# The up projection of an fp32 decoder trunk: seven products for two of every three tile pairs instead of one of two, the norm's factor moved, loops written out

## The reference, cut to what matters

```
x  = x + merged @ w_o                      # the stage before the change
h2 = rmsnorm(x) * g_ffn
f_gate, f_up = split(h2 @ w_up)            # 1024 -> 2 x 2816, the changed stage
f  = causal_depthwise_conv3(f_gate)        # along tokens
x  = x + (silu(f) * f_up) @ w_down         # the stage behind it
y  = rmsnorm(x) * g_final                  # rmsnorm(x) = x / sqrt(mean(x*x) + 1e-6)
```

## Time and profile before

| what | value |
|---|---|
| median of the runs | 860.32 us |
| the profiled execution's own time | 860.38 us |
| its span, first to last instruction | 858.4 us |
| PE busy | 844.3 us, 98% |
| DVE busy | 662.1 us, 77% |
| ACT busy | 400.2 us, 47% |
| TensorE clock granted, mean | 0.995 |
| up projection on PE | 478.21 to 722.98 us of the span |
| down projection | from 722.98 us |

### The profile page before, as it was taken

The page is one execution under the profiler, slowest core; times in us unless marked ns, Lnnn a source line. Parts: engine busy times, 40 slices in busy tenths (PEclk is TensorE's granted clock), DMA queues, the critical chain, the costliest instruction groups (busy, mean ns, idle before and its releaser), DMA issues.

```text
span 858.4 us, 19038 instructions
## 1 busy us (share of the span) xinstructions
PE 844.3 (98%) x6984; PEld 840.9 (98%) x6984; DVE 662.1 (77%) x994; ACT 400.2 (47%) x696; POOL 129.0 (15%) x98
## 2 busy tenths in 40 slices
PE   8999999999999999999999989999999999999996
PEld 7999999999999999999999989999999999999996
DVE  5899998999999966665689888888888888634334
ACT  8754646364332235662246644444444447432232
POOL 2283837474000000000013100000000000000000
PEclk9999999999999999999999999999999999999998
DMA  8433233433332333219822133333333332454433
GB/s 257 129 90 103 75 99 96 143 92 99 111 105 80 92 109 99 74 49 157 186 75 73 50 97 99 95 96 94 95 97 95 97 97 83 128 134 99 91 77 113
DMA packets 189144, 88.68 MB, mean 103 GB/s; under 512 B 34758, under 2 KB 187644, under 8 KB 189076
## 3 DMA queue, kind: packets, MB, share of 16 engines
q1 hardware_dynamic: 186225, 86.29, 37.1%
q10 hardware_dynamic: 2875, 1.82, 0.7%
HBM read 83.79 MB, written 3.51 MB: 102 GB/s over the span
## 4 chain that ended last, share of the span: by engine, by line
PE 95%; DVE 3%; ACT 1%; issue 1%; ACTq 0%; DVEq 0%
PE psum L1618 43%; PE psum L1624 21%; PE psum L1820 9%; PE psum L1792 8%; PE psum L1825 4%; PE psum L1797 4%; PE psum L1929 1%; PE psum L1938 1%; PE psum L1661 1%; PE psum L1668 0%; PE psum L1659 0%; DVE u L1235 0%; PE psum L1596 0%; DVE act L1017 0%; DVE w_lo L1013 0%
## 5 line engine op out<-in xcount | busy, mean ns | idle before, releaser
L1618 PE MATMUL psum<-act,w_hi 128*128 128x260 f32 x2600 | 341.4, 282 | 0.4 <-DVE act L1017 0.4
L1618 PEld LDWEIGHTS psum<-act,w_hi 128*128 128x128 f32 x2600 | 323.1, 188 | 0.8 <-DVE act L1017 0.6
L1013 DVE TENSOR_TENSOR w_lo<-raw,w_hi 128x1024 fp32r<-128x1024 f32 (+2 forms) x110 | 129.9, 1183 | 80.3 <-ACT w_hi L502 79.9
L1624 PE MATMUL psum<-act,w_lo 128*128 128x260 f32 x1300 | 185.1, 282 | 0.0
L1624 PEld LDWEIGHTS psum<-act,w_lo 128*128 128x128 f32 x1300 | 168.2, 188 | 0.0
L502 ACT ACTIVATE w_hi<-raw 128x1024 fp32r<-128x1024 f32 (+2 forms) x110 | 107.1, 977 | 89.2 <-PE psum L1624 81.8
L470 POOL TENSOR_TENSOR gate_a<-gate_a,prods 128x512 f32<-128x512 f32 x72 | 110.1, 1529 | 79.6 <-ACT prods L587 71.2
L1820 PE MATMUL psum<-act,w_hi 128*128 128x260 f32 x528 | 89.5, 282 | 0.9 <-ACT w_hi L773 0.9
L1820 PEld LDWEIGHTS psum<-act,w_hi 128*128 128x128 f32 x528 | 76.8, 188 | 1.1 <-ACT w_hi L773 1.1
L1090 DVE SCALAR_TENSOR_TENSOR psum<-u,cst,psum 128x512 f32<-128x512 f32 x96 | 66.8, 746 | 0.0
L1618 PE MATMUL psum<-mid,w_hi 128*128 128x260 f32 x512 | 66.5, 282 | 0.0
(11 more groups left out here) (212 smaller groups left out, 1081.5 us busy)
## 6 DMA issues: line engine op xcount, KB each, us to landing
raw<-in_w_in SPq DMA_DIRECT2D x56, 512.0 KB, 3.9
raw<-in_w_up SPq DMA_DIRECT2D x44, 512.0 KB, 3.9
raw<-in_w_down SPq DMA_DIRECT2D x16, 384.0 KB, 3.6
raw<-in_w_down SPq DMA_DIRECT2D x16, 320.0 KB, 3.0
v<-in_x_prompt SPq DMA_DIRECT2D x8, 512.0 KB, 7.2
raw<-in_w_b_out SPq DMA_DIRECT2D x8, 512.0 KB, 3.7
raw<-in_w_a_out SPq DMA_DIRECT2D x8, 512.0 KB, 5.8
raw<-in_w_o SPq DMA_DIRECT2D x8, 512.0 KB, 4.5
```

Source lines behind the costliest of these rows:

```text
L1013: ve.tensor_tensor(w_lo[:, slot, 0:k, :], raw[:, s, 0:k, :], w_hi[:, slot, 0:k, :], ALU.subtract).then_inc(lo_done, 1)
L1618: pe.matmul(a[:, h, :], w_hi[:, s, j, :], rhs(k, part)[:, h * H:(h + 1) * H], start=start and part == 0, stop=False)
L1624: last = pe.matmul(a[:, h, :], w_lo[:, s, j, :], rhs(k, 0)[:, h * H:(h + 1) * H], start=False, stop=stop)
```

## The change

Two of every three pairs have seven products now: pairs n with n % 3 > 0, 14 instead of 11, so that a plain pair is followed by a first and a second one with seven products (`SECOND[n]`). The second ones use other PSUM banks (`bank_x`, `banks_zy`), and P4 of the first one runs inside the second one, behind its P1. All loops of this stage are written out, on PE, ACT, DVE and SP, and waits are on constants. The two adds for the gate tile become one on 520 columns (`up_gate`, which needs P3 done). The elementwise work of tile n-1 lies in step n.

The up branch does not get the norm's factor any more: `gain` is gone. Its results are too large by the root of the mean square, and so is the down projection's sum, so x is multiplied by that root (`x_times_root`, 8 DVE instructions of 128x520 in the down stage), and the final norm, which divides it out, gets its epsilon times the root squared (`turn_root`, once, at pair 6, which brings the root from one row per token into one value per partition). The 8 sample columns of the convolution begin with a copy on ACT, and DVE's third conv instruction goes into the second, which is 520 wide.

At the stage's start `hi_up(0)` and the split of the sum of squares come before three token splits, `lo_open(1)` stands before the wait for the root, and the first `up_1` before `conv_first`. At its end the last pair is plain, and the splits for the down projection stand in another order.

```diff
-    DOWN_SLOT = (1, 2, 0, 3)
+    DOWN_SLOT = (2, 0, 1, 3)
+    SEVEN = [n % 3 > 0 for n in range(FT)]
...
-        snap_1, snap_v, snap_5 = uf[:, s2_at + N:s2_at + N + H], tmp[:, 2, 0:H], tmp[:, 2, H:N]
+        snap_1, snap_v, snap_5 = tmp[:, 2, 0:H], tmp[:, 2, H:N], uf[:, s2_at + N:s2_at + N + H]
         c22 = up_n[:, 0:H]
+        x_root_row = ssum
+        root_blocks, root_last, root_turned = up_n[:, H:H + P], up_n[:, H + P:H + P + Q], up_n[:, H + P + Q:H + P + 2 * Q]
+        eps_scaled = stat[:, 24:24 + TT + 1]
...
+        SECOND = [n > 0 and SEVEN[n] and SEVEN[n - 1] for n in range(FT)]
...
+        def bank_x(n):
+            return psum[:, 2 if SECOND[n] else 3, 0:H]
+
+        def banks_zy(n):
+            return psum[:, 4:6, 0:H] if SECOND[n] else psum[:, 6:8, 0:H]
...
                     b_hi_split("B22", j)
-                    b_hi_split("T2", j)
                     square_x(i)
-                    b_hi_split("T3", j)
-                    b_hi_split("T4", j)
+                    if i == KT - 1:
+                        hi_up(0)
+                        sum_hi_split(2, ssum, ssum_done, START + 2 * KT)
+                    for name in ("T2", "T3", "T4"):
+                        b_hi_split(name, j)
...
+            def up_1(n):
+                sc.wait_ge(p_done, PRODUCT["P1", n])
+                if NTH[n] > 0:
+                    sc.wait_ge(c1_set, NTH[n])
+                sc.activation(snap_1, bank_x(n), ACT.Copy).then_inc(snap, 1)
+
+            def up_v(n):
+                sc.wait_ge(p_done, PRODUCT["P6", n])
+                sc.activation(snap_v, bank_x(n), ACT.Copy).then_inc(snap, 1)
...
+                sc.activation(t0[:, SEQ:N], cst_f[:, i, 0:B * PADB:PADB], ACT.Copy).then_inc(tap_0, 1)
...
+            def plain_step(n):
+
+                if n > 0:
+                    conv_first(n - 1)
+                    hi_up(n)
+                    silu(n - 1)
+                hi_open(n + 1)
+                if 0 < n <= EARLY_HI:
+                    up_hi(n - 1)
...
-                    sc.activation(rinv, rinv, ACT.Sqrt).then_inc(var_root, 1)
+                    sc.activation(x_root_row, rinv, ACT.Sqrt).then_inc(var_root, 1)
...
+            def seven_step(n):
+
+                hi_4(n)
+                if SECOND[n] or n == 1:
+                    up_1(n)
+                    conv_first(n - 1)
+                else:
+                    conv_first(n - 1)
+                    up_1(n)
+                hi_3(n)
+                hi_open(n + 1)
+                silu(n - 1)
+                up_v(n)
+                up_5(n)
+                if n <= EARLY_HI:
+                    up_hi(n - 1)
+                if SEVEN[n + 1]:
+                    hi_2(n + 1)
...
+            def up_gate(n):
+                ve.wait_ge(p_done, PRODUCT["P3", n])
+                ve.wait_ge(snap, 3 * NTH[n] + 2)
+                conv_in_free(n)
+                ve.tensor_tensor(halves(cx[:, PADB:PADB + N]), banks_zy(n), halves(tmp[:, 2, :]), ALU.add).then_inc(c1_set, 1)
...
-            def gain(i):
-
-                ve.wait_ge(silu_done, START + i + 1)
-                ve.tensor_tensor(t1, t1, rinv, ALU.mult).then_inc(gain_set, 1)
-                ve.wait_ge(gain_set, i + 1)
...
-                ve.scalar_tensor_tensor(out=t0[:, SEQ:N], in0=cx[:, PADB + SEQ:PADB + N], scalar=scal(cst_f, i, CF_W + PADB),
-                                        in1=cst_f[:, bass.ds(i, 1), 0:B * PADB:PADB].rearrange("p o b -> p (o b)"),
-                                        op0=ALU.mult, op1=ALU.add).then_inc(conv_f, 1)
...
+            def turn_root():
+
+                for a in range(P // Q):
+                    rows = slice(a * Q, (a + 1) * Q)
+                    ve.transpose(root_blocks[rows, :], x_root_row[rows, 0:SEQ].rearrange("p (t b c) -> p b t c", t=TT, c=Q)[:, a]).then_inc(root_turn, 1)
...
+                ve.scalar_tensor_tensor(out=eps_scaled[:, 0:TT], in0=root_blocks[:, 0:P:Q], scalar=RMS_EPS, in1=root_blocks[:, 0:P:Q],
+                                        op0=ALU.mult, op1=ALU.mult).then_inc(eps_set, 1)
...
+            def plain_step(n):
+
+                if n > 0:
+                    up_gate(n - 1)
+                weight_sums(n + 1)
+                if n > 0:
+                    conv_rest(n - 1)
+                    lo_up(n)
+                    up_product(n - 1)
+                else:
                     root_eps(2, square_banks, RMS_EPS)
...
+                lo_open(n + 1)
+                if n == 0:
+                    ve.wait_ge(var_root, 2)
+                    ve.reciprocal(rinv, x_root_row).then_inc(rinv_done, 1)
+                    ve.wait_ge(rinv_done, 2)
+                    lo_2(n + 1)
+                weight_sum_4(n + 1)
+                if 0 < n <= EARLY_HI:
+                    up_lo(n - 1)
+                if n > 0:
+                    lo_2(n + 1)
+                if n == 6:
+                    turn_root()
+
+            def seven_step(n):
+
+                if SECOND[n]:
+                    lo_2(n)
+                    up_gate(n - 1)
+                    lo_4(n)
+                    lo_3(n)
+                    conv_rest(n - 1)
+                else:
+                    plain_gate(n - 1)
+                    lo_4(n)
+                    conv_rest(n - 1)
+                    lo_3(n)
+                lo_open(n + 1)
+                if SEVEN[n + 1]:
+                    weight_sums(n + 1)
+                if SECOND[n]:
+                    up_product(n - 1)
+                else:
+                    plain_product(n - 1)
+                up_22(n)
+                if SEVEN[n + 1]:
+                    weight_sum_4(n + 1)
+                if n <= EARLY_HI:
+                    up_lo(n - 1)
...
+            def x_times_root(n):
+
+                ve.tensor_tensor(tile(xT, n), tile(xT, n), x_root_row, ALU.mult).then_inc(x_by_root, 1)
...
-            ve.tensor_scalar(ms, stat[:, 18:18 + TT + 1], 1.0 / D, RMS_EPS, ALU.mult, ALU.add).then_inc(y_stat, 1)
+            ve.wait_ge(eps_set, 2)
+            ve.scalar_tensor_tensor(out=ms, in0=stat[:, 18:18 + TT + 1], scalar=1.0 / D, in1=eps_scaled, op0=ALU.mult,
+                                    op1=ALU.add).then_inc(y_stat, 1)
...
+                if n > 2:
+                    pe.wait_ge(prod_done, START + 2 * KT + n - 2)
+                product("P1", n)
+                if SECOND[n]:
+                    fourth(n - 1)
+                    pe.wait_ge(prod_done, START + 2 * KT + n - 1)
+                elif n == 1:
+                    pe.wait_ge(var_eps, 2)
+                else:
+                    pe.wait_ge(c1_set, NTH[n] - 1)
+                product("P2", n)
+                pe.wait_ge(snap, 3 * NTH[n] + 1)
+                product("P6", n)
+                product("P5", n)
+                pe.wait_ge(snap, 3 * NTH[n] + 2)
+                product("P7", n)
+                pe.wait_ge(snap, 3 * NTH[n] + 3)
+                product("P3", n)
```

More of the change, by code:

```diff
@@ L802, in hi_4 @@
[L802 to L811 removed]
+                    sc.wait_ge(p_done, PRODUCT["P4", n - 1])
+                hi_slot(3, s)
@@ L886, in plain_step @@
                     sc.wait_ge(var_eps, 2)
-                    sc.activation(rinv, rinv, ACT.Sqrt).then_inc(var_root, 1)
+                    sc.activation(x_root_row, rinv, ACT.Sqrt).then_inc(var_root, 1)
                     sc.activation(rs, ms, ACT.Silu).then_inc(table_set, 1)
-                hi_2(a, first)
-            def seven_step(a, split, first=False, last=False):
-                hi_4(a, first)
-                conv_first(2 * a)
-                up_1(a, first)
-                hi_3(a)
-                if last:
-                    down_hi(0, p_of(a, P2))
-                else:
-                    hi_gate(a + 1)
-                silu(2 * a)
-                up_v(a, first)
-                up_5(a, first)
-                if split:
-                    up_hi(2 * a)
@@ new lines, in _ @@
+            for n in range(FT - 1):
+                if SEVEN[n]:
+                    seven_step(n)
+                else:
+                    plain_step(n)
+            conv_first(FT - 2)
+            for i in range(EARLY_HI, EARLY_HI + 2):
+                up_hi(i)
+            hi_up(FT - 1)
+            silu(FT - 2)
+            down_hi(0, PRODUCT["P5", FT - 2])
+            down_hi(1, PRODUCT["P3", FT - 2])
+            for i in range(EARLY_HI + 2, EARLY_HI + 6):
+                up_hi(i)
@@ L1487, in _ @@
+            for i in range(EARLY_HI + 2, EARLY_HI + 4):
+                up_lo(i)
             conv_rest(FT - 1)
```

451 lines of the change are left out of this document (205 added, 246 removed).

## The result

The changed kernel takes **867.27 us** (median of 6 runs, 866.33 to 870.85) where the kernel before takes 860.3 (860.09 to 861.06): a ratio of **1.0088, 95% interval 1.0068 to 1.0108**, slower by more than the 0.2% that can be told here. The forecast was 864.6, with 856.0 to 869.5 as its range.

What follows compares the result with a forecast made beforehand. The prediction took PE, busy in 98% of the span, as the bound: -4.32 (matmuls) - 3.78 (start) + 12.73 (seven second-pair waits) - 0.41 (end) = +4.22 on 860.38, giving 864.6 us, range 856.0 to 869.5.

Steps and rivals of the forecast that it cites:

- Fewer matmuls: Whole stage on PE: three pairs change from 96 to 84 matmuls, 36 x 0.120 us, so -4.32.
- The wait in the second pair: P7 of every second pair: PE waits 1.30 us for `up_v`; pairs 11, 14, 17 and 20 give 5.20.
- the walk: Step-by-step timing of DVE and ACT from a plain pair's start: P7 can start at 30.10, due at 28.80.
- Pairs 5 and 8: Second pairs with extra DVE work: waits of 1.96 (`up_hi`, `up_lo` in between) and 2.18 (`turn_root` ahead, 1.4 to 3.5).
- The start: Stage's start up to the end of its P3: P6 waits 2.2 instead of 3.7, P7 another 0.70; in all -3.78.
- Pair 2: First of the seven second pairs: inherits the stage's start, so P7 starts at 512.36 instead of 508.97, 3.39 us.
- The end: First down unit at the stage's end: the last unit's wait of 0.4 goes, -0.41.
- the floor: Second pairs, rival: DVE's lag isn't there, only the least wait of 0.63 in each of seven; 856.3 us, chance 0.22.
- half the lag: Second pairs, rival: waits of 1.0 in each and 2.2 in pair 2; about 860.0 us, no change, chance 0.13.
- The clock rival: Behind the new waits: the clock falls as after the 3.7 us wait, 1.6 for each of six; 874 us, chance 0.06.
- its lag: DVE running late in second pairs; sign: only without it DVE waits for ACT before `lo_3`, and PE's waits are 0.6.
- the rule against the change: DVE's late chain: the next instruction waits for an empty pipe, 0.09 at each of eight starts; sum about 869.5.

Runs made afterwards that it cites:

- experiment 1: Changed kernel with ACT issuing `up_v` and `up_5` ahead of `silu` in second pairs: 852.96 us, ratio 0.9911 to the kernel before.
- experiment 2: Changed kernel with DVE doing the rest of the convolution ahead of `lo_3` in second pairs: 854.22 us, ratio 0.9926 to the kernel before.
- experiment 4: Changed kernel with `turn_root` moved from tile 6 to the stage's end: 866.01 us, ratio 1.0062 to the kernel before.
- experiment 8: Kernel before without its DVE instruction per tile that multiplies by the norm's factor: 859.57 us, ratio 0.9983 to the kernel before.
- experiment 3: Changed kernel plus one 128x520 DVE instruction per tile where the factor had been multiplied: 875.89 us, ratio 1.0171 to the kernel before.
- experiment 5: Experiment 1's kernel with ACT, in tile 1 alone, issuing `up_1` ahead of `hi_4` and `up_v` ahead of `silu`: 852.84 us, ratio 0.991.
- experiment 9: Kernel before with ACT issuing `up_1` ahead of `hi_4` and `conv_first` in the first pair alone: 859.88 us, ratio 0.9993.
- experiment 6: Experiment 5's kernel with ACT's and DVE's orders at the stage's start changed further, mainly for tile 1: 851.62 us, ratio 0.989.

## Why the prediction was right

The mechanism, its places and its sign were as forecast: PE waits for `up_v` at P7 of every second pair, and experiments 1 and 2 take that wait away at two places of the chain. The size was low: +7.0 measured for +4.2. The sum by its own terms, with what the trace shows (a wait's cost is taken as the time of its products less 0.120 for each matmul):

- *Fewer matmuls, -4.32.* As said: 1948 for 1984, at 0.120 throughout, written out or not. The 13 packets more on the instruction queue cost nothing to be seen.
- *The wait in the second pair, 4 x 1.30.* The row has 1.27, in four pairs alike, and each step of the walk is there: from the end of `up_gate` to `lo_3` 1.95 (642.24 to 644.19), from `lo_3` to P7 3.68 (644.19 to 647.87), as walked. The price was 1.58. The step that fell short took the time from due to start and left out that the first matmuls behind a wait are slower (0.11); the rest is the walk up to `up_gate`, above all the stretch from the first pair's `lo_3` (633.61 to 640.82 is 7.21, walked 7.07). 4 x 0.28 is 1.1 too little.
- *Pairs 5 and 8*, 1.96 and 2.18: 2.19 and 2.43. Of that `turn_root` 0.85 against 0.9 (experiment 4); on DVE it takes 2.05 (561.89 to 563.94) where 2.1 was taken.
- *The start, -3.78.* P6 waited for `up_1` as forecast, 2.48 in the row and 2.63 in cost where I had 2.2, P7 0.62 (0.70), and P6 of pair 2 another 0.57 that I did not have: -2.88. The wait before P6 came out longer because DVE reached `root_eps` at 488.27, 0.5 later than walked (487.28) once the stage's later start is taken off. Pair 2 then cost 2.95 instead of 3.39; together 6.77 for 6.31.
- *The end, -0.41.* The first down unit takes 15.82 for 16.79: -0.97, of which about 0.7 is the wait that experiment 8 removes.
- *Not in the sum*: the stage starts 0.46 later in this execution (478.67 for 478.21). Experiments 1, 2 and 4 have the same code ahead of it and start within 0.05 of the kernel before, so it is not the change.

-4.32 - 2.88 + 13.9 (2.95 + 2.19 + 2.43 + 6.30) - 0.97 + 0.46 = +6.2, against 6.3 measured between the two spans. The prediction had +4.22; half of the rest is the price of a wait. The other misses partly cancel (the start 0.9 and pairs 5 and 8 0.5 too low, pair 2 0.4 and the end 0.6 too high), and that the sum came within 2.1 owes something to it.

The rivals: the floor and half the lag fall by the waits (1.27 where they need 0.3 to 1.0). The clock rival fell in the profiled run and was right in part in others: 867.84 to 870.85 at a clock of 0.995 to 0.991 would be 1 to 3 falls of 1.5 by their size, for these runs have no trace; the median lies 0.6 over the profiled run. I had argued that a wait of 1.3 is nearer to 0.9, which shows no fall, than to 3.7; that holds for the four late waits, where no profiled run of 1.27 shows one. Pair 2's wait is of a length behind which the clock fell elsewhere (2.44 in experiment 4, 2.68 in experiment 3), so I should have given it a price of its own. Whether a fall came behind pair 5's 1.88 or pair 8's 2.12 isn't shown.

One indicator was wrong as I wrote it. DVE was to wait for ACT before `lo_3` of a second pair "only if its lag is gone"; it does wait, 1.34, with PE's wait at 1.27. My own walk had that wait in it (free at 25.08, `hi_3` at 26.40). So the lag sat in `up_gate`, which DVE reached late, and not in `lo_3`. The other signs came as said (a cycle of 33.26 for 33.0, DVE at 26.0 and not over 27), but for `up_1`, which PE waited for twice (2.48 and 0.27) and not once.

What the prediction didn't ask is why `up_v` had to come behind `silu`. It priced the order as given; the walk shows in one line that `up_v` needs nothing of it.

In the changed trace `lo_3` at 644.19 is 1.23 long and the next, independent instruction starts at 645.33, 0.09 before its end. So the late chain is to be summed by starts, as the prediction did. The time alone would not tell: 867.27 lies between the 864.6 by the rows and the 869.5 by the rule against the change. The Trainium skill, VectorE: DVE Perf Modes, section on the DRAIN you can't avoid, has the next instruction wait until the pipe is empty, and adds that one which nothing holds back starts earlier. The prediction took only the first half; the trace agrees with the second.

## What to carry to other kernels

When an engine's order puts a short copy that another engine waits for behind a long chain, walk the copy's own inputs: if they were there long before, moving the copy is worth the whole wait and needs nothing else (three calls, 14 us). Take from a steady cycle's period, not from the idle row, what a wait costs. And where TensorE is late for a short while, look first for the next event that another engine's own program sets. Up to there, a wait taken away, or a slow clock, changed next to nothing (experiments 5 and 9), and the time moved when that engine's order was changed as well (experiment 6).
